# Holding back row gathers by three places instead of six and ten

## The reference

```python
        a = jnp.einsum('chkd,cd->chk', u_tab[eidx], xc)
        wgt = (jax.nn.gelu(a.astype(jnp.float32)) * g).astype(xc.dtype)
        return jnp.einsum('chk,chkd->cd', wgt, v_tab[eidx])
```

## Time and profile before

| | us |
|---|---|
| median of 3 runs | 1711.26 |
| lowest, highest | 1709.15, 1712.77 |
| profiled execution, first to last instruction | 1783.7 |

### The profile page before, as it was taken

One profiled execution on the slowest core, in us unless ns is written; L12 is line 12 of the kernel. 1 busy time (PEld: TensorE's weight loads), 2 busy tenths in 40 slices (PEclk: granted clock), 3 DMA queues, 4 the chain that ended last, 5 costly groups with the idle time before them and its releaser, 6 DMA issues.

```text
span 1783.7 us, 18187 instructions
## 1 busy us (share of the span) xinstructions
PE 1504.7 (84%) x6234; PEld 833.2 (47%) x6234; DVE 882.4 (49%) x2004; ACT 319.5 (18%) x647; POOL 505.8 (28%) x540
## 2 busy tenths in 40 slices
PE   8989999999999999999999987576767676767667
PEld 6856554434343434478757776232322222322222
DVE  3986143222232323452153697766665657562744
ACT  3113222111010101301230111321111111120110
POOL 3000000000000000000000254757676767676764
PEclk9999989999999999999999987788788888888889
DMA  9686746999999999942302296999898999999997
GB/s 332 238 296 236 291 149 262 424 429 427 428 429 429 428 428 429 390 143 108 129 1 83 76 379 242 394 354 409 334 396 338 400 342 390 356 379 352 397 355 278
DMA packets 135278, 565.40 MB, mean 317 GB/s; under 512 B 11497, under 2 KB 17430, under 8 KB 122732
## 3 DMA queue, kind: packets, MB, share of 16 engines
q1 hardware_dynamic: 60588, 295.66, 41.4%
q0 software_dynamic: 74416, 268.84, 39.3%
q10 hardware_dynamic: 208, 0.09, 0.0%
HBM read 563.49 MB, written 1.06 MB: 317 GB/s over the span
## 4 chain that ended last, share of the span: by engine, by line
PE 77%; issue 10%; DMA 5%; DVE 4%; POOL 2%; ACT 2%; another core or an unknown queue 0%; ACTq 0%; DVEq 0%; POOLq 0%
PE psum L409 53%; PE psum L1018 21%; DMA ring<-in_peer_v_dram,attnT 2%; POOL ring L1164 2%; DMA ring<-in_peer_u_dram,attnT 1%; DMA dft<-in_peer_v_dram,attnT 1%; PE psum L760 0%; DVE arena L1650 0%; PE psum L766 0%; PE psum L417 0%; DMA tok<-in_peer_u_dram,attnT 0%; DVE spec L1653 0%; DVE ring L1974 0%; DVE scratch L1973 0%; DVE ring L1972 0%
## 5 line engine op out<-in xcount | busy, mean ns | idle before, releaser
L1018 PE MATMUL psum<-ring,arena 128*128 128x512 f32 x772 | 380.4, 643 | 182.3 <-issue 91.1
L409 PE MATMUL psum<-ring,arena 128*64 128x512 f32 (+1 forms) x1552 | 343.8, 594 | 1.4 <-DVE arena L1833 1.4
L1018 PEld LDWEIGHTS psum<-ring,arena 128*128 128x128 f32 x772 | 155.8, 204 | 403.2 <-issue 317.3
L1164 POOL DMA_INDIRECT dft<-in_peer_u_dram,attnT x10 | 9.5, 950 | 1002.7 <-DVE attnT L2098 998.6
L2128 DVE CUSTOM_DVE_ANT_0 scratch<-ring,psum 128x1024 f32<-128x1024 f32 x216 | 254.8, 1218 | 65.3 <-DMA ring<-in_peer_u_dram,attnT 48.7
L409 PE MATMUL psum<-actT,ring 128*128 128x256 f32 (+1 forms) x1424 | 267.7, 349 | 22.1 <-issue 18.6
L409 PEld LDWEIGHTS psum<-actT,ring 128*128 128x128 f32 x1424 | 238.8, 197 | 51.4 <-issue 28.3
L1164 POOL DMA_INDIRECT ring<-in_peer_u_dram,attnT x216 | 205.5, 951 | 159.8 <-issue 64.5
L1164 POOL DMA_INDIRECT ring<-in_peer_v_dram,attnT x218 | 211.2, 969 | 72.5 <-issue 62.5
L409 PEld LDWEIGHTS psum<-ring,arena 128*64 128x64 f32 (+1 forms) x1552 | 110.4, 137 | 219.4 <-issue 206.0
L1451 ACT ACTIVATE arena<-ident,attnT 128x128 f32<-128x128 f32 x226 | 80.5, 395 | 393.1 <-PE psum L1018 149.9
(11 more groups left out here) (390 smaller groups left out, 1434.8 us busy)
## 6 DMA issues: line engine op xcount, KB each, us to landing
ring<-in_w_gate_dram SPq DMA_DIRECT2D x32, 2048.0 KB, 12.3
ring<-in_w_up_dram SPq DMA_DIRECT2D x32, 2048.0 KB, 16.6
ring<-in_w_down_dram SPq DMA_DIRECT2D x32, 2048.0 KB, 13.8
ring<-in_w_in_dram SPq DMA_DIRECT2D x15, 2048.0 KB, 14.9
ring<-in_ada_w_dram SPq DMA_DIRECT2D x12, 2048.0 KB, 10.2
ring<-in_w_out_dram SPq DMA_DIRECT2D x4, 2048.0 KB, 7.8
ring<-in_peer_wq_dram SPq DMA_DIRECT2D x4, 2048.0 KB, 8.1
ring<-in_w_attn_out_dram SPq DMA_DIRECT2D x2, 2048.0 KB, 12.1
```

The costliest lines, as they stand in the source:

```text
L409: return nc.tensor.matmul(o, lhsT, rhs, start=(k == 0), stop=(k == n - 1))
L1018: last = nc.tensor.matmul(psum[:, 4 + 2 * t + n, :], diag[:, i, :], rowbufs[b][:, n * 512:(n + 1) * 512], start=first, stop=final)
L1164: pool.indirect_dma_start(out=rowbufs[b], out_offset=None, in_=tab, in_offset=bass.IndirectOffsetOnAxis(ap=rowid[:, j // 4, k:k + 1], axis ...
```

## The change

`awaited(n)` names the gather that must have landed before gather n is issued. Before, it was gather n - 6 for the first 64 and n - 10 for the others; now it is gather n - 3 for all. Nothing else is changed: the same instructions, buffers and orders.

```diff
         def awaited(n):
 
-            m = n - (6 if n < 64 else 10)
+            m = n - 3
             return None if m < 0 else row_place(*TURNS[m // GROUP], m % GROUP)
```

## The result

The changed kernel takes 2048.1 us (median of 4 runs, 2045.2 to 2050.7), before 1710.5 us beside it: a ratio of 1.197 (95% interval 1.194 to 1.199), 337.6 us slower. The forecast was 1910 us, range 1795 to 2000. The direction was right, the size was not.

The account below looks back on a forecast made before the run. The pace of POOL's gathers was taken to bound the long stage. For the runs, 1711.3 + 461 x (1.72 - 1.264) = 1921.5 us, rounded down to 1910 for landings seen a little sooner; range 1795 to 2000 us.

Parts of the forecast that it names:

- The wait binds: At POOL's gathers: landing takes 4.35 to 5.58 us, over the 3.75 us of three issues, so nearly every gather waits.
- The new pace, 1.72 us: The 461 late gather steps: a 5.15 us round trip over three places, 1.72 us each, +138.1 us on the profile.
- The pace of before, 1.264 us: Late gather steps in the runs before: (1711.3 - 1111.3 - 17.6) / 461 = 1.264 us each.
- The first 50 gathers covered: Early gathers: at most 23.5 us more, against 28.9 us of POOL's bank waits; the issue at 1111.32 stays within 5 us.
- The crawl: Long gather stage: all engines slow while transfers run at 409 GB/s, making readers late; 65 us, likeliest only in the profile.
- The tail: Behind the last gather's issue: 17.6 us, perhaps 1 us shorter after the change, left as it is.
- B: Rival for the long gather stage: round trip longer yet, 1.98 us a step gives 2041 us, 1.86 gives 1986; 13%.
- A: Rival: the engines' slowness at 409 GB/s is in the runs too, so +138.1 us carries over to 1849 us; 17%.
- C: Rival: no change, POOL sees landings sooner than VectorE, round trip under 3.84 us; 1711 us; 4%.
- D: Rival: faster, fewer transfers end the engines' slowness while pace holds, round trip under 4.26 us; down to 1646 us; 4%.
- The 72 us: Profiled execution over the runs' median, 1783.7 against 1711.26; 65 us placed in the long gather stage, likeliest that execution's own.
- The signs that I named: Profile after: gathers 1.6 to 1.85 us apart, POOL idle 0.6 to 0.9 us, 290 to 330 GB/s, gather 50 near 1111.

## Why the prediction was wrong, point by point

**The wait binds: right.** A landing takes longer than the 3.75 us of three issues: 5.2 us by the median after, 4.2 even alone. The estimate of 3.2 us by the Trainium skill ("DMA: Bandwidth & Descriptors", section "Anatomy of one DMA — SWDGE (gpsimd) path") does not hold for these gathers.

**The new pace, 1.72 us: wrong, and this is the step that failed.** As I put it: "three places take one round trip from issue to the release of the engine that waits", and "I take gather 418's 5.15 us". The 5.15 was near the round trip to VectorE (5.95 - 0.63 = 5.32 measured), but it ended at VectorE's release, and the engine that waits is POOL. POOL starts 0.63 us behind VectorE on the same row, and with the waits in the other order 0.13. The term was mis-sized by 5.95 - 5.15 = 0.80 us for three places, 0.265 for each, 122 us in all; 97 of these (461 x 0.63 / 3) are POOL's own delay, the rest a longer landing. Of the 97, the run with the waits in the other order gave back 47, and would have given 77 had the landing stayed as it was.

**The pace of before, 1.264 us: wrong.** It came from subtracting 1111.3 us, most likely one chip's, from another chip's 1711. With ten places the pace is 1.295 us where before takes 1711. That makes the loss 461 x 0.031 = 14 us smaller than I reckoned.

**The first 50 gathers covered: wrong.** The cover of 28.9 us belonged to the slower chip, where the projections are late too. Elsewhere, with the same six places, it is 7.6 us, and gather 50 moves from 1091.2 to 1117.9, 26.7 us. I had allowed 5.

**The crawl comes with transfers at 409 GB/s: wrong.** The runs show 409 GB/s without it and 207 GB/s with it.

**The sum, mended.** 1921.5 + 122 - 14 + 27 - 5 = 2051.5, the 5 being the tail, 16.3 for 21.0. The profiled run took 2050.7 us, the median is 2048.1. Put together from the traces, the span of before is 1091.2 + 461 x 1.295 + 21.0 = 1709 and that of after 1117.8 + 914.9 + 16.3 = 2049; a run's time is 1.8 us more than its span.

**Nothing is late next: right.** TensorE waits 421.3 us for v rows, and the small instructions are not held up. **The tail: right for after**, 16.3 us from the last issue; I had not seen that before has some 21 where it takes 1711.

**The rivals.** *B* named the right pace, 1.98 us, and 2041 us, at 13%, by chance: its 5.95 us was a round trip with five in flight, and the runs with fewer and with more in flight show that no round trip is fixed. *A* (the difference carries over) is close only in form: where the slow-down is, the loss is 2051.9 - 1790.2 = 262 us, not 138. *C* and *D* needed a round trip under 3.84 and 4.26 us; it is 5.95, and 5.05 even with one gather in flight. The 72 us were neither the one profiled execution's own, as I had taken for likeliest, nor in all runs alike; that every run of some chips has them was not among my cases. The signs that I named hold for the span (2048.9, with a median of 2048.1), the tail and the short instructions, and fail for gather 50, the pace, POOL's idle time (1.05 us a gather) and the 290 GB/s.

## What to carry to other kernels

With k transfers in flight the pace is (landing + the issuer's own delay) / k until the queue or the issue rate takes over; here that needs six (within half a per cent of ten), and each place taken away from six costs more than the one before. Measure the delay at the engine that will wait: another engine was released by the same semaphore 0.63 us earlier, which is 97 us over the stage. And if a profile's span is several per cent off the runs' median, subtract nothing across the two before the same chip has shown both.

## What the runs showed of the hardware

- The same row's landing starts VectorE 0.63 us ahead of POOL's gather where the landing wait is the second of POOL's two waits, and 0.13 us ahead where it is the first. What POOL does in the half microsecond no row shows.
- A gather of 128 rows of 4 KB lands 4.2 us after its issue begins when alone, 5.2 with two others in flight; of 2 KB rows with two others 3.5.
- On two of five chips every run of the kernel before took 4.3 to 4.6% longer than on the others. In their traces the short instructions that pick a group's rows are stretched from 9 us to as much as 47 while POOL issues gathers at 1.25 us, and no landing of a gather is recorded; halving the bytes does not help, and issuing each 1.98 us does. The cause was not found, and the recording itself is not ruled out.
